# Moving the shared expert's down product behind the first expert pair's gate and up products, and loading some expert weights in halves

## What is computed

```
def moe_ffn(h, w_router, router_bias, w_gate, w_up, w_down, ws_gate, ws_up, ws_down):
    ...
    wts = wts / jnp.sum(wts, -1, keepdims=True) * ROUTED_SCALE
    ...
    def expert_block(args):
        e, tok, wr = args
        xb = h[tok]
        y = (jax.nn.silu(xb @ w_gate[e]) * (xb @ w_up[e])) @ w_down[e]
        return y * wr[:, None].astype(h.dtype)
    ...
    routed = jax.ops.segment_sum(ys.reshape(R, D), row_tok, num_segments=N)
    shared = (jax.nn.silu(h @ ws_gate) * (h @ ws_up)) @ ws_down
    return routed + shared
```

## Time and profile before

| | |
|---|---|
| median of 3 runs | 2257.49 us (2256.29 to 2257.75) |
| profiled execution | 2254.97 us |
| its span, first to last instruction | 2253.2 us |
| PE busy | 98% of the span |
| DVE, ACT busy | 52%, 31% |
| DMA, mean rate over the span | 282 GB/s |
| mean granted TensorE clock | 0.995 |

### The profile page before, as it was taken

How to read it: one execution, slowest core, us unless ns; L and a number is a source line. 1 busy time by engine, 2 the same in 40 slices (tenths; PEclk the granted TensorE clock), 3 DMA queues, 4 the chain that set the end, 5 groups by cost and what they waited for, 6 DMA issues and landing times.

```text
span 2253.2 us, 32105 instructions
## 1 busy us (share of the span) xinstructions
PE 2212.9 (98%) x12584; PEld 1594.2 (71%) x12584; DVE 1160.9 (52%) x1461; ACT 692.3 (31%) x761; POOL 12.6 (1%) x28
## 2 busy tenths in 40 slices
PE   8999999999999999999999999999999999999996
PEld 8899999999978888888887954444444444444442
DVE  6457576666766445454556733333444444334435
ACT  4343434334344333333344411111111111111112
POOL 1000000000000000000000000000000000000000
PEclk9999999999999999999999999999999999999998
DMA  7444434444445555555666399999999999999996
GB/s 284 150 172 157 159 132 167 143 155 158 148 173 198 186 191 200 186 188 194 234 225 251 145 384 428 427 428 427 428 428 428 429 429 428 428 429 428 428 427 278
DMA packets 62178, 635.37 MB, mean 282 GB/s; under 512 B 7424, under 2 KB 7552, under 8 KB 10384
## 3 DMA queue, kind: packets, MB, share of 16 engines
q1 hardware_dynamic: 60192, 627.30, 69.5%
q0 software_dynamic: 752, 4.75, 0.6%
q10 hardware_dynamic: 1152, 2.10, 0.3%
HBM read 632.02 MB, written 2.10 MB: 281 GB/s over the span
## 4 chain that ended last, share of the span: by engine, by line
PE 75%; DMA 18%; DVE 3%; issue 1%; ACT 1%; SPq 0%; DVEq 0%; ACTq 0%
PE bank L305 27%; PE bank L273 18%; DMA wgu<-wgu 17%; PE bank L856 13%; PE bank L904 5%; PE bank L531 4%; PE bank L804 3%; PE bank L814 3%; DMA raw<-units 1%; DVE kk L1495 1%; PE bank L766 1%; DMA wdt_raw<-wdt 1%; DVE wlo L1232 1%; PE bank L837 0%; DVE wlo L1569 0%
## 5 line engine op out<-in xcount | busy, mean ns | idle before, releaser
L1232 DVE TENSOR_TENSOR wlo<-raw,whi 128x2048 fp32r<-128x2048 f32 x185 | 424.0, 2292 | 370.0 <-ACT whi L952 366.9
L952 ACT ACTIVATE whi<-raw 128x2048 fp32r<-128x2048 f32 x185 | 354.3, 1915 | 436.1 <-PE bank L305 344.9
L856 PE MATMUL bank<-wgu,xg 128*64 128x512 f32 x2048 | 448.9, 593 | 4.1 <-DMA wgu<-wgu 4.1
L856 PEld LDWEIGHTS bank<-wgu,xg 128*64 128x64 f32 x2048 | 145.5, 137 | 300.7 <-issue 281.8
L273 PE MATMUL bank<-xhi,whi 128*128 128x256 f32 x896 | 260.5, 291 | 2.3 <-DVE wlo L1232 2.3
L273 PE MATMUL bank<-xhi,wlo 128*128 128x256 f32 x896 | 253.4, 283 | 0.0
L273 PE MATMUL bank<-xlo,whi 128*128 128x256 f32 x896 | 253.4, 283 | 0.0
L904 PE MATMUL bank<-wd,eactT 128*64 128x512 f32 x1024 | 226.8, 595 | 0.0
L1749 DVE SCALAR_TENSOR_TENSOR eact<-eth,bank 128x256 f32<-128x256 f32 x32 | 13.5, 422 | 364.8 <-issue 192.9
L305 PE MATMUL bank<-whi,xhi 128*128 128x512 f32 x512 | 199.8, 390 | 0.0
L305 PE MATMUL bank<-whi,xlo 128*128 128x512 f32 x512 | 199.3, 389 | 0.0
(11 more groups left out here) (364 smaller groups left out, 3327.9 us busy)
## 6 DMA issues: line engine op xcount, KB each, us to landing
wgu<-wgu SPq DMA_DIRECT2D x128, 2048.0 KB, 21.6
raw<-units SPq DMA_DIRECT2D x204, 1024.0 KB, 4.8
wd<-wd SPq DMA_DIRECT2D x64, 2048.0 KB, 18.7
raw<-units SPq DMA_DIRECT2D x6, 512.0 KB, 6.9
stage<-units SPq DMA_DIRECT2D x2, 1024.0 KB, 13.2
h<-xtok POOLq DMA_DIRECT2D x2, 1024.0 KB, 8.7
out<-acc SPq DMA_DIRECT2D x3, 512.0 KB, 2.6
stage<-units SPq DMA_DIRECT2D x2, 512.0 KB, 9.4
```

Source lines behind the costliest of these rows:

```text
L856: mi = nc.tensor.matmul(bank[3][CAP * j:CAP * j + CAP, :], buf[:, 4 * c + k, CAP * (2 * half + j):CAP * (2 * half + j + 1)], wgu_t[c][:, j ...
L952: nc.scalar.activation(whi[u % SPLIT][:, :], raw[u % RAW][:, :], ACT.Copy).then_inc(hi_done, 1)
L1232: V.tensor_tensor(wlo[u % SPLIT][:, :], raw[u % RAW][:, :], whi[u % SPLIT][:, :].bitcast(f32), ALU.subtract).then_inc(lo_done, 1)
```

## The change

1. PE does the shared down product after the first pair's gate and up product instead of before it, then waits for all eight adds (`acc_ok`).
2. DVE makes `pick`, the first slot weights and `rounds_ok` before the shared adds instead of after them.
3. In the first pair (`opening`), the four gather blocks stand behind the down product, in banks 6 and 7; ACT and DVE copy them there.
4. `wgu0`, `wd0` and `wd1` are loaded as two transfers of 1 MB (rows of 8 KB per partition instead of 16 KB), each with a semaphore of its own, and PE releases them in halves. `wgu1` to `wgu3` stay whole. The arrays in memory are laid out so that each half is contiguous per partition.
5. Semaphores are merged: `wdt_raw` counts on `par_in`, and ACT's split of it waits for 80, which is all five small loads; four semaphores of the merge stage become one counter.

```
-        sp.dma_start(wdt_raw[:, :], wdt).then_inc(dt_in, 16)
+        sp.dma_start(wdt_raw[:, :], wdt).then_inc(par_in, 16)
...
         def load_down(pair, it):
-            for c in range(2):
+            for c, h in ((0, 0), (0, 1), (1, 0), (1, 1)):
                 if it is not None:
-                    sp.wait_ge(ex["d_free"] if c == 0 else ex["y_ps"], (it if c == 0 else it * 4) + START)
-                elif c == 1:
+                    sp.wait_ge(ex["d_free"] if c == 0 else ex["y_ps"],
+                               (it * 2 + (h - 1) if c == 0 else it * 4 + (2 * h - 2)) + START)
+                elif (c, h) == (1, 0):
                     sp.wait_ge(sh["lo_ok"], 1)
-                sp.dma_start(wd_t[c][:, :, :], wd[pair, c]).then_inc(d_full[c], 16)
+                sp.dma_start(wd_t[c][:, h, :, :], wd[pair, c, :, h]).then_inc(d_full[c][h], 16)
 
         def load_pair(it, pair):
 
-            for c in range(4):
-                sp.wait_ge(ex["gu_free"], it * 4 + (c - 3) + START)
+            for h, full in enumerate((gu_full[0], gu0_rest)):
+                sp.wait_ge(ex["gu_free"], it * 5 + (h - 4) + START)
+                sp.dma_start(wgu_t[0][:, 2 * h:2 * h + 2, :, :], wgu[pair, 0, :, 2 * h:2 * h + 2]).then_inc(full, 16)
+            for c in range(1, 4):
+                sp.wait_ge(ex["gu_free"], it * 5 + (c - 3) + START)
                 sp.dma_start(wgu_t[c][:, :, :, :], wgu[pair, c]).then_inc(gu_full[c], 16)
             load_down(pair, it)
...
-        pe.wait_ge(sh["lo_ok"], 1)
-        for j in range(2):
...
+        def shared_down(pe):
+
+            pe.wait_ge(sh["lo_ok"], 1)
+            for j in range(2):
...
                 for c in range(4):
-                    pe.wait_ge(gu_full[c], it * 16 + 16)
                     for k in range(4):
+                        if k == 0:
+                            pe.wait_ge(gu_full[c], it * 16 + 16)
+                        if c == 0 and k == 2:
+                            mi.then_inc(ex["gu_free"], 1)
+                            pe.wait_ge(gu0_rest, it * 16 + 16)
...
                 else:
+                    shared_down(pe)
                     pe.wait_ge(sh["acc_ok"], 8)
                     pe.sem_inc(ex["sc_ps"], 8)
+                opening = first and u == 0
...
-                        if f == 0 and c == 3:
+                        if f == 0 and c % 2 == 1:
                             mi.then_inc(ex["d_free"], 1)
                         if f == 1:
                             mi.then_inc(ex["y_ps"], 1)
+                if opening:
+                    for j in range(4):
+                        gather_block(4 * half + j, j, (6, 7), it * 2 + (4 + j // 2))
...
-        act.wait_ge(dt_in, 16)
+        act.wait_ge(par_in, 80)
         nc.scalar.activation(wdt_hi, wdt_raw[:, :].rearrange("p (k h) -> p k h", h=16), ACT.Copy).then_inc(dt_w, 1)
```

More of the change, by code:

```diff
@@ L207, in build_trunk @@
     rcnt = at("rcnt", 207.3125, [P, 4])
-    wgu_t = [at(f"wgu{c}", (0, 16, 160, 176)[c], [P, 2, 4, 2 * FE]) for c in range(4)]
-    wd_t = [at("wd0", 128, [P, 2, D]), at("wd1", 112, [P, 2, D])]
+    wgu_t = [at(f"wgu{c}", (0, 16, 160, 176)[c], [P, 4, 2, 2 * FE]) for c in range(4)]
+    wd_t = [at("wd0", 128, [P, 2, 2, D // 2]), at("wd1", 112, [P, 2, 2, D // 2])]
     xg = [at(f"xg{j}", 40 + 16 * j, [P, KT, Q4]) for j in range(2)]
@@ L383, in _ @@
             sp.wait_ge(unit_used, N_S0 + c + 1 - N_X)
-            sp.dma_start(wgu_t[c][:, :, :, :], wgu[0, c]).then_inc(gu_full[c], 16)
+            if c == 0:
+                for h, full in enumerate((gu_full[0], gu0_rest)):
+                    sp.dma_start(wgu_t[0][:, 2 * h:2 * h + 2, :, :], wgu[0, 0, :, 2 * h:2 * h + 2]).then_inc(full, 16)
+            else:
+                sp.dma_start(wgu_t[c][:, :, :, :], wgu[0, c]).then_inc(gu_full[c], 16)
         load_down(0, None)
@@ L884, in four_pairs @@
                 mi.then_inc(ex["at_ps"], 1)
-                if gathers:
+                if gathers and not opening:
                     gather_block(4 * half + 3, 3, (0, 1), it * 2 + 5)
@@ L1182, in four_pairs @@
                 buf, half = 1 - u // 2, u % 2
-                act.wait_ge(ex["gu_free"], it * 4 + 4 + START)
+                act.wait_ge(ex["gu_free"], it * 5 + 5 + START)
                 nc.scalar.activation(eth[:, :], bank[3][:, 0:FE], ACT.Tanh, scale=0.5).then_inc(ex["th_ok"], 1)
-                if not (last and u >= 2):
+                opening = first and u == 0
+                if not (last and u >= 2) and not opening:
                     for j in (0, 2):
@@ L1202, in four_pairs @@
                                          scale=wslot[:, :]).then_inc(ex["y_ok"], 1)
+                if opening:
+                    for j in (0, 2):
+                        gathered(buf, 4 * half + j, j, 6, it * 4 + 8)
         four_pairs(0, True, False)
@@ L1760, in four_pairs @@
                 else:
+                    shared_out()
+                    dve.wait_ge(sh["acc_ok"], 8)
                     dve.sem_inc(ex["acc_ok"], 8)
-                if gathers:
+                opening = first and u == 0
+                if gathers and not opening:
                     gathered(buf, 4 * half + 1, 1, 1, it * 4 + 8)
@@ L1778, in four_pairs @@
                                            yehi[:, sl].bitcast(f32), ALU.mult, ALU.subtract).then_inc(ex["y_split"], 1)
+                if opening:
+                    for j in (1, 3):
+                        gathered(buf, 4 * half + j, j, 7, it * 4 + 8)
                 if not (last and u == 3):
```

79 lines of the change are left out of this document (42 added, 37 removed).

## The result

The changed kernel took 2266.21 us (median of 6 runs, 2261.97 to 2267.67), the kernel before 2257.34 us beside it (6 runs, 2254.38 to 2257.75). The ratio is 1.0041, with an interval of 1.0031 to 1.0051: **slower by 7.0 to 11.5 us**. Forecast were 2259.2 and a range that ended at 2264.0. The profiled execution lasted 2267.67 us, with a span of 2265.9.

The account below looks back on a forecast made before the run. The prediction took the expert loads, at their limit of 428 GB/s, to set the end. Head start -1.41, toll of halves +2.4 and merged semaphore +0.67 gave +1.7 on 2257.49, so 2259.2 us, range 2254.5 to 2264.

Parts of the forecast that it names:

- The toll of halves: In the expert loads, 1 MB halves at 426 GB/s cost 0.085 us a pair, +2.4 us over 28 pairs.
- rival of the larger toll: Expert loads in halves run at 421 GB/s, +7.2 us, sum +6.5, 2264.0 us; chance 14%.
- head start: At the hand-over to the experts, loads restart without the 5.80 us gap; later pauses leave 1.41 us gain.
- The pause ahead of the down chunks: In the first pair, the loads stand empty for 0.87 us before the first down half.
- The merged semaphore: In the opening, ACT's split of wdt_raw waits for all five small loads, +0.67 us.
- The clock: Rival: PE's clock falls at the new gaps or the longer early one, +1.5 us, sum +3.2, 2260.7; chance 12%.
- theory B: Formed after the result: the opening causes the loss, by merged semaphore and longer half clock, +2.2 us.

Follow-up runs that it names:

- e13: Kernel before with 32 KB rows for the first two gate chunks and both down chunks, each pair of chunks loaded jointly, from pair 4 to pair 30: 2252.93 us, ratio 0.9986.
- e10: Kernel before with all four gate and up chunks loaded as two loads of 4 MB from pair 2 on: 2256.72 us, ratio 0.9999.
- e9: Kernel before with the first two gate and up chunks loaded as one load of 4 MB from pair 2 on: 2257.37 us, ratio 1.0004.
- e3: Changed kernel with whole loads in place of halves and the old separate semaphore, so the new order alone: 2259.36 us, ratio 1.0010.
- e12: Kernel before with first gate chunk and both down chunks each loaded as two loads to every second partition, rows still 16 KB: 2255.73 us, ratio 0.9997.
- e6: Kernel before with as many loads, but 16 KB rows of the first gate chunk and both down chunks moved as two of 8 KB: 2263.26 us, ratio 1.0031.
- e4: Kernel before with the first gate chunk and both down chunks loaded in halves, old order, separate semaphore for wdt_raw: 2262.52 us, ratio 1.0031.
- e8: As e4, with gate chunks 1 to 3 loaded in halves too, both halves behind one wait and one semaphore: 2270.01 us, ratio 1.0060.
- e11: As e6, with rows of 4 KB for the first gate chunk and both down chunks: 2276.05 us, ratio 1.0091.
- e5_order_gathers_kept: As e3, but the first pair's four gather blocks stay where the kernel before has them: 2257.61 us, ratio 1.0002.
- e2_merged_sem_only: Kernel before with only the merged semaphore, wdt_raw counting on par_in: 2256.87 us, ratio 1.0003.
- e1_own_sem: Changed kernel with the small load wdt_raw given a semaphore of its own again: 2264.78 us, ratio 1.0036.
- e14: The same program as e3 run again, the new order with whole loads and the old semaphore: 2257.59 us, ratio 1.0005.
- e15_before_again: The kernel before, unchanged, run once more for a second trace: 2258.35 us.
- e7: Kernel before with first gate chunk and both down chunks each loaded as two loads to 64 neighbouring partitions, rows still 16 KB: 3040.95 us, ratio 1.3476.

## Why the prediction was wrong

The periods side by side, read from the chains, settle the cause:

| kernel | loads a pair | rows a pair | period us | GB/s |
|---|---|---|---|---|
| e13 | 4 | 512 | 29.21 | 431 |
| e10 | 4 | 512 | 29.23 | 431 |
| e9 | 5 | 640 | 29.29 | 430 |
| before, e3 | 6 | 768 | 29.37 | 428 |
| e12 | 9 | 768 | 29.37 | 428 |
| e6 | 6 | 1152 | 29.60 | 425 |
| e4, after | 9 | 1152 | 29.59 | 425 |
| e8 | 12 | 1536 | 29.81 | 422 |
| e11 | 6 | 1920 | 30.04 | 419 |

From 768 to 1920 rows the period grows by 0.67 us: **0.58 ns a row**, whatever the number of loads; the 256 rows fewer of e10 and e13 take off 0.14 to 0.16. If one of the 16 DMA engines carries a row while the others carry theirs, that is 16 x 0.58 = 9.3 ns of an engine's time for every row, an estimate. The records of the single packets in the traces, 1850 to 2120 us, have the toll too: a row of 16 KB took 614.7 ns on its engine (the kernel before), one of 8 KB 313.6 (e8), so two of 8 KB take 12.5 ns more than one of 16 KB. Why this is 3 ns more than the periods give isn't shown; the records overlap a little (a DMA share of 1.01 in the windows).

**The toll of halves: the step that failed.** "At 426 2.462, at 423 2.479. I take 426, the purer stretch: 0.014 per half" gave 0.085 us a pair and +2.4 us. Measured are 0.22 us a pair, 0.037 per half, and +5.7 us in D (e4_halves_only). A stream of nothing but such halves runs at 422 GB/s (e8_all_chunks_halved), so both rows of the trace read high, and the one that was set aside as impure was the nearer. The windows of 4 and 12 us were too short for a difference of 1.5%: the prediction named that weakness and still priced by it. The size was inside its own bounds (0 to +7.2); only the choice between them was wrong. In its toll, what happened is the rival of the larger toll (14%). Between the forecast sum of +1.7 us and the 8.0 us summed up below lie 6.3 us: 3.7 are this toll (+6.1 to the last down product, for +2.4), 1.7 the head start (+0.3 for -1.41) and 0.9 the late wait. With the toll alone put right the forecast is 2257.49 - 1.41 + 6.1 + 0.67 = 2262.9, still inside the range; with +0.3 in the place of the head start's -1.41 as well it is 2264.6, outside. So the head start is the second step that failed.

**The head start: right mechanism, nothing left of 1.41 us.** The first half of this step held: first gate and up product 0.84 us behind G (forecast 0.78), empty stretch gone, three pauses in place. Two terms were off. The pause ahead of the down chunks was forecast at 0.87 us: loads from G + 30.15 out of work, issue at G + 29.33. Measured: out of work near 1330.0, G + 29.1, and issue at 1331.22, G + 30.30, with 1.69 of start-up some 2.9 us. The stream ran dry earlier because it had been further ahead at G, which costs nothing in itself. What costs is that PE was later than worked out: pair 1 at G + 39.37 against 36.27, so 3.10 us, not 2.07. The 1.03 us more are in the chain above: the add 1.01 for 0.78, two transposes 0.42 and 0.44 for 0.22 each, the shared product 11.12 for 10.91, the gathers 4.11 for 4.01, and 0.05 and 0.07 at the first product, less 0.07 at ACT's copy (1.01 by these rounded figures). From there the forecast pauses moved along: the down load of pair 2 is issued at 1364.37, G + 63.45, forecast 1357.78, G + 62.22. These 1.23 us are nearly all of the 1.41. In D the order then costs 0.1 to 0.3 us with halves and 0.4 to 0.6 with whole loads. That sum of pauses and D agree no better than to some half a microsecond; e5_order_gathers_kept shows it, where PE came 0.94 us earlier and D didn't shrink.

**The merged semaphore: right at its place.** `wdt_split` moved from 28.90 to 29.54, and PE's product behind it from 35.50 to 36.13. The two traces with the merged semaphore have that product at 36.11 and 36.13, the fifteen others at 35.43 to 35.52. PE's idle time ahead of it, 1.82 us where it was 0.93, is no measure of this: with the old semaphore it ranges from 0.69 (e3_order_only) to 2.10 (e4_halves_only) and is 1.75 in the second trace of the kernel before. Whether 0.65 us reach the end isn't resolved (e2_merged_sem_only: +0.6, interval -1.4 to +2.7). In the merge stage three semaphores became one counter, not four; no run isolates it.

**The clock: right not to count it.** It stayed at 1.00 in the windows of the bare waits, as above from 1306 on. In the opening the mean granted clock over 34 to 70 us was 0.86 in the changed kernel and 0.91 in the kernel before, which theory B was built on. But it was 0.86 in the second trace of the kernel before too, and 0.81 in e1_own_sem, with the old semaphore: this differs from execution to execution, and B falls away.

**Not foreseen: the late wait.** 0.9 us at pair 29. It is in the changed kernel, e3, e14, e10 (0.9 to 1.3 us), e1 (1.5) and, at pair 30, e9 (0.8), and neither in two traces of the kernel before nor in e2, e4, e5, e6, e8, e11, e12 and e13. It came again with the same program (1.24 and 1.25 us of idle time in e3 and e14), so it seems to belong to the program more than to the execution; two traces can't prove that. The new order isn't its condition, since e9 and e10 have the old one. The stream shows no pause there. What the traces do show is a step in how the loads land. Each load raises its semaphore 16 times, and PE goes on after the sixteenth. In e14 the sixteenth comes 2.22 us behind the first for every load up to G + 848 and 3.50 us from the next load on, with the last one alone 1.29 behind the fifteenth. Between the two begins, at 2144.3 (G + 847.7), a packet of 16 KB of the instruction queue, 1.1 us long. The changed kernel (3.00 to 3.85, packet at G + 853.1), e1 (3.34 to 4.83), e3 (2.36 to 3.37), e10 (3.03 to 4.14) and e9 (3.45 to 4.27, at its second such packet, G + 872.0) have the same step at the same place. In the traces without a late wait such a packet lies there as well, but the sixteenth signal hardly moves: 3.42 to 3.54 in the kernel before, 3.38 to 3.49 in e15_before_again. So one sixteenth of the stream falls behind at that packet and doesn't catch up, and PE feels it only where that share was already among the last. Which DMA engine a packet ran on isn't in the traces, so this cause fits in all six and stays an inference, and why it hits the last share in some programs is open.

**The sum as measured:** halves +6.1 from G to the last down product (e4), order +0.3, late wait +0.9, semaphore +0.65 at its place ahead of G: 8.0 us, inside the measured 7.0 to 11.5. The spans of the two traces differ by 12.7 us, but 5.4 of it lie ahead of G, where the same program came out 3.4 us apart (e15_before_again).

## What to carry to other kernels

Where a full stream of loads sets the end, count the rows that it moves before anything else: the number of loads was free, each row cost, and so the way to split a load is by partitions that alternate, and the way to speed up the stream is longer rows, as long as PE doesn't have to wait for the larger pieces at the end (e9 and e10 had the shorter period and gained nothing, e13 kept single chunks there). Price such a toll from a window of hundreds of microseconds or from the period of a repeated stage, never from a few microseconds of another stage. A head start that has to be kept in single buffers is worth only what PE's own lateness leaves of it, so every wait that a moved step used to cover belongs into the sum at full length.

## What the runs showed of the hardware

- **A row costs some 9 ns on its DMA engine** over its bytes, from 4 to 32 KB alike: 9.3 ns estimated from the periods, 12.5 from the packets' records. Carried to no rows at all, 29.37 - 768 x 0.00058 = 28.92 us for 12.58 MB are 435 GB/s. The Trainium skill, "SBUF — State Buffer", section "Door 1: The DMA port swizzle", gives the same 435 GB/s as the limit of the ports; no run here reached it, the closest was 431.
- **Loads of 64 neighbouring partitions moved 208 GB/s** with the DMA engines 97% busy (e7), loads of every second partition 428 (e12). The Trainium skill, "SBUF — State Buffer", section "Door 1: The DMA port swizzle", says why: partitions 0 to 63 reach only 8 of the 16 ports. By its table every second partition reaches all 16, and the trace agrees.
- **A full queue doesn't charge for more loads**: 12 loads of 1 MB a pair (e8) lie on the same line of rows as 6 loads (e11, e6). The Trainium skill, "SBUF — State Buffer", section "The DMA setup-cost knee (why "@ 1 MiB" ≠ asymptote)", charges about 2 us for every transfer; in a full queue the trace shows none of it, e12 with three more loads a pair has the same 29.37 us.
